# A decoder step with paged latent attention on one core: tiles that take a quarter of every page, and scales turned by VectorE

## The chip, the cores and the metric

The kernel runs on one core of a Trainium2 chip. The metric is the time of one execution on the device in microseconds (us). Everything is float32. Engines are named as in the profile: PE is TensorE (PEld its weight loads), DVE is VectorE, ACT is ScalarE, POOL is GpSimd, SP is SyncE, whose queue issues most DMAs.

## The reference

One step of a one-layer decoder serves 512 prompt tokens and 8 sample sequences of 4 tokens. It has two groups of heads: latent attention (MLA) and an RWKV-7 delta rule. The change touches only the attention of the sample tokens over a paged cache of latent rows:

```python
def _sample_attention(qn, qp, kn_new, kp_new, v_new, cache_ckv, cache_kpe, layer, page_table, w_ukv, g_kn):
    def step(carry, phys):
        c_blk = cache_ckv[layer, phys]
        kp_blk = cache_kpe[layer, phys]
        kn_blk, v_blk = _decompress(c_blk, w_ukv, g_kn)
        return _merge(carry, _attn_partial(qn, qp, kn_blk, kp_blk, v_blk, None)), None

    carry, _ = lax.scan(step, init, page_table.T)
```

`_decompress` multiplies a page's 128 latent rows of 256 numbers with `w_ukv` and normalises each head's 64 key numbers by their root mean square. A score is (query . normalised key + query . rotary key) x scale. The result is a softmax over 4096 cached and 4 new tokens, so the order of the tokens of a page does not matter, as long as all its users agree on it.

## The kernel before

The work over the cache ("page work") is 64 steps, `u`, each of four pages (512 tokens); eight steps in a row belong to one sequence. A step is cut in four slots, `t` = 0 to 3, and each engine has a generator (`pages_sp`, `pages_pool`, `pages_pe`, `pages_act`, `pages_dve`) that yields after each slot. The other work of the kernel (delta-rule chunks, sequence work, latent projections, prompt attention) calls `on_pe.go(n)`, `on_dve.go(n)` and so on between its own operations, which puts n slots of page work there into that engine's program. So the order on every engine is fixed by where `go` stands and by what a generator does in which slot; engines meet only at semaphores. 17 x 4 slots lie beside the chunks, 24 beside the sequence work, 35 beside the latent work, 34 beside the prompt attention (8 heads of four query tiles), and the last 91 run alone.

The way of one step:

- SP loads the pages into `c_ring` (`latent_pages`, L441), partition = token of the page; four steps fit the ring. From step 40 on POOL gathers two of the four pages (L489). SP waits for the landing, then copies 32 x 64 pieces into `blocks` (`blocks_of`, L451), half 0 (pages 0 and 1) and half 1 (pages 2 and 3), four copies each. A half is copied when its last transpose is done (`lo_sb`, `hi_sb`).
- DVE turns each half in 32x32 blocks into `c_T` (`turned_blocks`, L673): "lo" is half 0 (semaphore `lo_sb`), in slot 3 of the step before; "hi" is half 1 (`hi_sb`), in slot 0 of the step itself. It also turns the rotary keys `r_T` (L681, slot 1).
- PE computes the keys of one tile of 128 tokens per slot (`norms`, L563; tile t is page t), ACT squares them in PSUM (L609), DVE sums the squares per head (`reduce`, L686). `norms` of slot 0 waits for lo, that of slot 2 for hi, each for the sum two slots back.
- In slot 1 PE forms the dot products (`dots`, L526 with `r_T`, L530 with `c_T`), which wait for hi, and the value products of step u-2 (`values`, L547). ACT copies the latent part of the scores to SBUF (`dotted`, L604, slot 1).
- In slot 0 of the next step ACT and DVE make the 1/rms scales (`roots`, `scales`); DVE spreads them over `rep` (L696), in slot 2 PE turns them (`turn_scale`, L538), and DVE multiplies and adds (`score`, L705 to L712, slot 2). ACT takes the exponentials in slot 3 (`weights`, L624), PE turns them in slot 0 (L542), and DVE merges in slot 1 (`merge`, L718).

The norms are two matmuls a slot; a float32 matmul leaves two records in the trace, so a slot's norms are four records. The slots of VectorE (L726 to L738):

```python
            for u, t in slots:
                ahead = u + 1 < NSTEP
                if t == 0:
                    if u >= 1:
                        turned_blocks(u, 1)
                        scales(u - 1)
                if t == 1 and u >= 2:
                    merge(u - 2)
                if t == 2 and u >= 1:
                    score(u - 1)
                if t == 3 and ahead:
                    turned_blocks(u + 1, 0)
                reduce(u, t)
```

## Time and profile before

| | us |
|---|---|
| runs before: median of 3 (lowest, highest) | 1276.44 (1276.27, 1277.88) |
| the profiled execution's own time | 1276.86 |
| its span in the profile | 1275.1 |
| PE busy in the span | 1202.1 (94%) |
| DVE busy | 732.2 (57%) |
| ACT busy | 426.5 (33%) |
| POOL busy | 257.4 (20%) |

The profile is one execution, recorded by the hardware. A group of instructions shows its line, engine, operation and tiles, its busy time and count, the mean length of one in ns, and the idle time of the engine before them with what ended it. "issue" there means that the profile shows nothing that was waited for. Matmuls are pipelined, so a record's length overlaps the next one's; what an instruction takes from PE is the distance between starts. The granted clock of PE is given as a share of its full 2.4 GHz.

### The profile page before, as it was taken

What the parts mean: (1) busy time and instruction counts of PE and PEld (TensorE: products, weight loads), DVE (VectorE), ACT (ScalarE), POOL (GpSimd) and SP (SyncE); (2) the same over time, 40 slices, a digit from 0 to 9 for tenths busy, and PEclk for the clock granted to TensorE, in tenths of its full rate; (3) what the DMA queues carried; (4) which work ended last, traced back from release to release, by engine and by line L of the source; (5) the groups of instructions that cost most, each with busy time, mean ns of one, the idle gap of its engine ahead of it and who ended that gap; (6) DMA issues with size and microseconds to landing.
All of it is one profiled execution on the core that took longest, in us unless ns stands there. A gap on an engine that the chain in (4) does not pass through costs nothing. (4 is left out here: it accounts for less than half of the span.)

```text
span 1275.1 us, 23690 instructions
## 1 busy us (share of the span) xinstructions
PE 1202.1 (94%) x8783; PEld 661.3 (52%) x8783; DVE 732.2 (57%) x1801; ACT 426.5 (33%) x1041; POOL 257.4 (20%) x294
## 2 busy tenths in 40 slices
PE   6999999989999999999989988999999999989898
PEld 3545677745565565655434445555444444454343
DVE  4000437955667666774768787888676667430331
ACT  3000354323343333342444343333444444210310
POOL 0000134711011121234412340001323232000000
PEclk9999999999999999997999999999999999999999
DMA  6413112123232222351453226532576544101000
GB/s 219 168 55 87 35 33 67 53 59 80 66 81 67 76 73 77 84 115 42 124 143 88 76 74 171 168 80 74 153 184 172 139 122 123 50 1 38 17 21 33
DMA packets 205236, 114.45 MB, mean 90 GB/s; under 512 B 152977, under 2 KB 196433, under 8 KB 204994
## 3 DMA queue, kind: packets, MB, share of 16 engines
q1 hardware_dynamic: 198482, 96.56, 27.7%
q0 software_dynamic: 4352, 10.49, 3.3%
q10 hardware_dynamic: 2288, 5.89, 1.3%
q8 instruction: 70, 1.15, 0.4%
q14 instruction: 44, 0.36, 0.1%
HBM read 75.79 MB, written 4.07 MB: 63 GB/s over the span
## 5 line engine op out<-in xcount | busy, mean ns | idle before, releaser
L563 PE MATMUL PS<-wk,c_T 128*128 128x512 f32 x1024 | 494.5, 612 | 13.5 <-DVE c_T L673 12.4
L563 PEld LDWEIGHTS PS<-wk,c_T 128*128 128x128 f32 x1024 | 180.3, 193 | 207.8 <-issue 162.8
L686 DVE TENSOR_REDUCE ssq<-PS 128x8 f32<-128x512 f32 x256 | 176.3, 689 | 169.7 <-ACT PS L609 156.8
L609 ACT ACTIVATE PS<-PS 128x512 f32<-128x512 f32 x256 | 150.3, 587 | 271.8 <-PE PS L563 245.0
L1557 PE MATMUL PS<-xnT,w_ring 128*128 128x276 f32 x416 | 101.0, 400 | 0.0
L1395 PE MATMUL PS<-w_ring,xnT 128*128 128x424 f32 x256 | 96.4, 534 | 0.9 <-DVE xnT L1041 0.9
L673 DVE STREAM_TRANSPOSE c_T<-blocks 128x512 f32<-128x512 f32 x126 | 88.3, 701 | 3.7 <-DMA blocks<-c_ring 3.2
L1557 PEld LDWEIGHTS PS<-xnT,w_ring 128*128 128x128 f32 x416 | 77.8, 190 | 20.6 <-issue 4.1
L489 POOL DMA_INDIRECT c_ring<-in_cache_ckv,token_rows x48 | 45.3, 944 | 182.1 <-PE PS L547 174.8
L480 POOL DMA_INDIRECT r_ring<-in_cache_kpe,group_rows x64 | 62.0, 969 | 92.3 <-DVE r_T L681 68.0
L1395 PEld LDWEIGHTS PS<-w_ring,xnT 128*128 128x128 f32 x256 | 48.8, 194 | 45.5 <-issue 45.4
L2791 PE MATMUL PS<-w_g,nT 128*128 128x512 f32 x128 | 56.1, 595 | 0.0
L1347 POOL TENSOR_TENSOR diff<-cur 128x512 f32<-128x512 f32 x13 | 17.2, 1322 | 181.0 <-DVE cur_s L1256 171.9
L1049 DVE COPY nat<-PS 128x424 f32<-128x424 f32 x8 | 4.8, 597 | 75.2 <-PE PS L1395 75.2
L3069 ACT ACTIVATE pr<-PS,mx 128x128 f32<-128x128 f32 (+3 forms) x32 | 16.9, 527 | 73.0 <-DVE mx L2919 63.7
L530 PE MATMUL PS<-c_T,qp 128*32 128x128 f32 x1024 | 40.8, 275 | 0.3 <-issue 0.3
L547 PE MATMUL PS<-c_ring,ew 128*32 128x257 f32 x512 | 40.0, 382 | 0.1
L2791 PEld LDWEIGHTS PS<-w_g,nT 128*128 128x128 f32 x128 | 24.0, 190 | 30.4 <-issue 30.4
L1892 POOL TENSOR_TENSOR low<-raw_l,cst 128x512 f32<-128x512 f32 x12 | 12.8, 1093 | 121.6 <-ACT raw_l L1847 121.6
L526 PE MATMUL PS<-r_T,q_rope 128*32 128x128 f32 x512 | 27.5, 286 | 8.8 <-issue 8.7
L718 DVE SCALAR_TENSOR_TENSOR acc<-acc,ms,PS 128x257 f32<-128x257 f32 x64 | 30.5, 477 | 8.6 <-PE PS L547 8.4
L624 ACT ACTIVATE ew_q<-score_s,ms 128x128 f32<-128x128 f32 x64 | 32.8, 512 | 0.0
(535 smaller groups left out, 1725.3 us busy)
## 6 DMA issues: line engine op xcount, KB each, us to landing
blocks<-c_ring SPq DMA_DIRECT2D x504, 64.0 KB
c_ring<-in_cache_ckv SPq DMA_DIRECT2D x208, 128.0 KB, 2.2
w_ring<-in_w_in SPq DMA_DIRECT2D x4, 1696.0 KB, 12.4
w_ring<-in_w_in SPq DMA_DIRECT2D x9, 512.0 KB, 5.1
w_o<-in_w_out SPq DMA_DIRECT2D x8, 512.0 KB, 4.9
w_g<-in_w_ple_gate SPq DMA_DIRECT2D x8, 512.0 KB
xn<-in_x_prompt SPq DMA_DIRECT2D x4, 512.0 KB, 10.9
w_ring<-in_w_in SPq DMA_DIRECT2D x2, 1024.0 KB, 6.1
```

Of the source, the lines that this page charges most:

```text
L480: nc.gpsimd.indirect_dma_start(r_ring[:, u % R_RING, :], None, rows_of, bass.IndirectOffsetOnAxis(ap=group_rows[:, j * BS + b:j * BS + b + ...
L489: nc.gpsimd.indirect_dma_start(c_ring[:, u % RING, x, 0:KVL], None, io["cache_ckv"].rearrange("n p c -> (n p) c"), bass.IndirectOffsetOnAx ...
L530: mm = pe.matmul(PS[t * QH:(t + 1) * QH, TURN, at + P:at + 2 * P], qp[:, k, u // STEPS, :], c_T[:, u % 2, k, t * P:(t + 1) * P], start=(k ...
L547: mm = pe.matmul(PS[t * QH:(t + 1) * QH, MISC, at_v], ew[:, t * QH:(t + 1) * QH], c_ring[:, u % RING, t, :], start=True, stop=True)
L563: mm = pe.matmul(PS[:, NORM[v % 2], :], c_T[:, u % 2, k, t * P:(t + 1) * P], wk[:, k], start=(k == 0), stop=(k == 1))
L609: nc.scalar.activation(PS[:, NORM[v % 2], :], PS[:, NORM[v % 2], :], ACT.Square).then_inc(no_sb, 1)
L624: nc.scalar.activation(ew_q[:].rearrange("x (p s) -> x s p", s=GT), score_s[:, u % 2, :].rearrange("x (s p) -> x s p", s=GT), ACT.Exp, bia ...
L673: dve.transpose(c_T[:, u % 2, :, 2 * half * P:2 * (half + 1) * P].rearrange("d x (t s p) -> d s t x p", t=2, s=GT), blocks[:, half, :].rea ...
L686: dve.tensor_reduce(ssq[:, u % 2, t * H:(t + 1) * H], PS[:, NORM[v % 2], :].rearrange("p (h c) -> p h c", h=H), AX.X, ALU.add).then_inc(re ...
L1395: mm = pe.matmul(PS[:, u % 4, 0:w], xnT[:, k, i * P:(i + 1) * P], w_ring[:, c % 2, k, 0:w], start=(k == 0), stop=(k == KD - 1))
L1557: mm = pe.matmul(PS[:, 2 * (p % 2) + part, 0:t1 - t0], w_ring[:, wc % 2, k, at_:at_ + P], xnT[:, k, t0:t1], start=(k == 0), stop=(k == KD ...
L2791: mm = pe.matmul(PS[:, g_bank(i) + half, :], nT[:, i % 2, k, :], w_g[:, k, half * 512:(half + 1) * 512], start=(k == 0), stop=(k == KD - 1))
```

## The change

A tile of 128 tokens is now 32 tokens of each of the four pages (quarter t of every page), not one page. For that a page is loaded so that partition p holds token p % 4 * 32 + p // 4, and the gathers' row numbers follow; `c_T` is laid out by quarter, so every tile needs both halves of `blocks`. With tiles by quarter the scales need only be turned within 32x32 blocks: DVE does it (`scale_T`) and `turn_scale` is gone, as is ACT's copy `dotted` (DVE reads the dots from PSUM). The keys `r_T` and the latent columns of `dots` are read through rearranged patterns to match.

In the slots: both transposes of `blocks` for step u+1 now lie in slots 2 (lo) and 3 (hi) of step u; `norms` of slot 0 waits for both; `dots` waits for neither. `score` moves from slot 2 to slot 1, behind `merge`; `weights` on ACT from slot 3 to slot 2. The slots of SP and POOL are as they were.

```diff
--- before.py
+++ after.py
@@ -99,7 +99,7 @@
     parts += [("seq", (s // TS == np.arange(BS)[None, :]))]
     parts += [("headsum", (s // HN == np.arange(2)[None, :]))]
     parts += [("headones", (s // HN == t // HN))]
-    parts += [("lane", s % 32), ("token", s)]
+    parts += [("lane", s % 32), ("token", s % 4 * 32 + s // 4)]
     parts += [("mod32", (s % 32 == t % 32))]
     parts += [("causal", np.where(t <= s, 0.0, NEG))]
 
@@ -250,7 +250,7 @@
         rms = place("rms", [P, 2, GT * H])
         ssq = place("ssq", [P, 2, GT * H])
         score_s = place("score_s", [P, 2, P])
-        rep = place("rep", [P, GT * QH])
+        scale_T = place("scale_T", [P, P])
         ew_q = place("ew_q", [P, P])
         ew = place("ew", [P, GT * QH])
         ms = place("ms", [P, 4])
@@ -412,9 +412,9 @@
 
 
         (slot_taken, k_ps, k_sb, tn_sb, rp_ps, no_ps, no_sb, red_sb,
-         ri_sb, scale_sb, scale_ps, np_sb, top_sb, al_sb, eq_sb, ew_ps, ew_sb, vv_ps, acc_sb, dve_a) = kept_sems(*(
+         ri_sb, top_sb, al_sb, eq_sb, ew_ps, ew_sb, vv_ps, acc_sb, dve_a) = kept_sems(*(
             "slot_taken k_ps k_sb tn_sb rp_ps no_ps no_sb red_sb "
-            "ri_sb scale_sb scale_ps np_sb top_sb al_sb eq_sb ew_ps ew_sb vv_ps acc_sb dve_a").split())
+            "ri_sb top_sb al_sb eq_sb ew_ps ew_sb vv_ps acc_sb dve_a").split())
         c_in = [kept_sems(*(f"c_in{half}{x}" for x in range(RING))) for half in "ab"]
         block_in = kept_sems("block_in_a", "block_in_b")
         late_in = kept_sems("late_in_a", "late_in_b")
@@ -439,7 +439,7 @@
         def latent_pages(u, page):
             for x, number in enumerate(page):
                 nc.sync.dma_start(c_ring[:, u % RING, x, 0:KVL],
-                                  io["cache_ckv"][bass.ds(number, 1)].rearrange("o p c -> (o p) c")
+                                  io["cache_ckv"][bass.ds(number, 1)].rearrange("o (s g) c -> (o g) s c", s=GT)
                                   ).then_inc(c_in[x // 2][u % RING], 16)
 
         def blocks_of(u, half):
@@ -497,10 +497,10 @@
                 return R_RING
             return min(NSTEP, slot // GT + R_RING) + max(0, min(NSTEP, (slot + 6) // GT + 1) - GATHERED)
 
-        def by_token(k):
-
-            return (c_T[:, 0, k, :].rearrange("d (t s p) -> d t s p", t=GT, s=GT),
-                    PS[:, TURN, :].rearrange("d (t p s) -> d t s p", t=GT, s=GT))
+        def by_quarter(k):
+
+            return (c_T[:, 0, k, :].rearrange("d (s t g) -> d t s g", s=GT, t=GT),
+                    PS[:, TURN, :].rearrange("d (t g s) -> d t s g", s=GT, t=GT))
 
         def pages_pe():
             pe = nc.tensor
@@ -517,28 +517,24 @@
 
             def dots(u):
                 pe.wait_ge(tn_sb, u + 1)
-                if u >= 1:
-                    pe.wait_ge(hi_sb, u)
                 if u >= 2:
                     pe.wait_ge(top_sb, u - 1)
                 at = u % 2 * 2 * P
                 for t in range(GT):
-                    pe.matmul(PS[t * QH:(t + 1) * QH, TURN, at:at + P], q_rope[:, u // STEPS, t, :], r_T[:],
+                    pe.matmul(PS[t * QH:(t + 1) * QH, TURN, at:at + P], q_rope[:, u // STEPS, t, :],
+                              r_T[:].rearrange("d (s g) -> d g s", s=GT),
                               start=True, stop=True)
                 for k in range(2):
                     for t in range(GT):
                         mm = pe.matmul(PS[t * QH:(t + 1) * QH, TURN, at + P:at + 2 * P], qp[:, k, u // STEPS, :],
-                                       c_T[:, u % 2, k, t * P:(t + 1) * P], start=(k == 0), stop=(k == 1))
+                                       c_T[:, u % 2, k, :].rearrange("d (q t i) -> d t q i", q=GT, t=GT)[:, t],
+                                       start=(k == 0), stop=(k == 1))
                 mm.then_inc(rp_ps, 1)
 
-            def turn_scale(u):
-                pe.wait_ge(scale_sb, u + 1)
+            def turn_weights(u):
+                pe.wait_ge(eq_sb, u + 1)
                 if u >= 1:
                     pe.wait_ge(acc_sb, u)
-                pe.transpose(PS[:, MISC, at_t], rep[:], ident).then_inc(scale_ps, 1)
-
-            def turn_weights(u):
-                pe.wait_ge(eq_sb, u + 1)
                 pe.transpose(PS[:, MISC, at_t], ew_q[:], ident).then_inc(ew_ps, 1)
 
             def values(u):
@@ -555,8 +551,7 @@
                         pe.wait_ge(k_sb, 2)
                     else:
                         pe.wait_ge(lo_sb, u)
-                if t == 2 and u >= 1:
-                    pe.wait_ge(hi_sb, u)
+                        pe.wait_ge(hi_sb, u)
                 if v >= 2:
                     pe.wait_ge(red_sb, v - 1)
                 for k in range(2):
@@ -575,15 +570,12 @@
                     dots(u)
                     if u >= 2:
                         values(u - 2)
-                if t == 2 and u >= 1:
-                    turn_scale(u - 1)
                 norms(u, t)
                 yield
             turn_weights(NSTEP - 2)
             yield
             values(NSTEP - 2)
             yield
-            turn_scale(NSTEP - 1)
             yield
             turn_weights(NSTEP - 1)
             yield
@@ -595,13 +587,7 @@
 
             def turned_first():
                 act.wait_ge(k_ps, 1)
-                nc.scalar.copy(*by_token(0)).then_inc(k_sb, 1)
-
-            def dotted(u):
-                act.wait_ge(rp_ps, u + 1)
-                if u >= 2:
-                    act.wait_ge(eq_sb, u - 1)
-                nc.scalar.copy(score_s[:, u % 2, :], PS[:, TURN, u % 2 * 2 * P + P:u % 2 * 2 * P + 2 * P]).then_inc(np_sb, 1)
+                nc.scalar.copy(*by_quarter(0)).then_inc(k_sb, 1)
 
             def square(u, t):
                 v = u * GT + t
@@ -640,9 +626,7 @@
                         turned_weights(u - 2)
                     if u >= 1:
                         roots(u - 1)
-                if t == 1:
-                    dotted(u)
-                if t == 3 and u >= 1:
+                if t == 2 and u >= 1:
                     weights(u - 1)
                 square(u, t)
                 yield
@@ -666,11 +650,11 @@
 
             def turned_first():
                 dve.wait_ge(k_ps, 2)
-                dve.tensor_copy(*by_token(1)).then_inc(k_sb, 1)
+                dve.tensor_copy(*by_quarter(1)).then_inc(k_sb, 1)
 
             def turned_blocks(u, half):
                 dve.wait_ge(block_in[half], 64 * u)
-                dve.transpose(c_T[:, u % 2, :, 2 * half * P:2 * (half + 1) * P].rearrange("d x (t s p) -> d s t x p", t=2, s=GT),
+                dve.transpose(c_T[:, u % 2].rearrange("d x (s t g) -> d s t x g", s=GT, t=GT)[:, :, 2 * half:2 * half + 2],
                               blocks[:, half, :].rearrange("p (s t c x) -> p s t x c", s=GT, t=2, x=2)
                               ).then_inc((lo_sb, hi_sb)[half], 1)
 
@@ -687,22 +671,20 @@
                                   AX.X, ALU.add).then_inc(red_sb, 1)
 
             def scales(u):
-                wide = [P, GT * H, TS]
                 y, tmp = rms[:, 0, :], rms[:, 1, :]
                 dve.wait_ge(ri_sb, u * 2 + 2)
                 LA(dve.tensor_tensor(tmp, y, y, ALU.mult))
                 LA(dve.scalar_tensor_tensor(out=tmp, in0=ssq[:, u % 2, :], scalar=EPS * NOPE, in1=tmp, op0=ALU.add, op1=ALU.mult))
                 LA(dve.tensor_scalar(tmp, tmp, -0.5 / NOPE, 1.5, ALU.mult, ALU.add))
-                dve.tensor_tensor(rep[:].rearrange("p (x t) -> p x t", t=TS),
-                                  y.rearrange("p (x o) -> p x o", o=1).to_broadcast(wide),
-                                  tmp.rearrange("p (x o) -> p x o", o=1).to_broadcast(wide), ALU.mult).then_inc(scale_sb, 1)
+                LA(dve.tensor_tensor(tmp, y, tmp, ALU.mult))
+                LA(dve.transpose(scale_T[:], tmp.rearrange("p (x o) -> p x o", o=1).to_broadcast([P, GT * H, TS])))
 
             def score(u):
                 nm, sc, at = nmax[:, u // STEPS:u // STEPS + 1], score_s[:, u % 2, :], u % 2 * 2 * P
                 dve.wait_ge(rp_ps, min(u + 2, NSTEP))
-                dve.wait_ge(np_sb, u + 1)
-                dve.wait_ge(scale_ps, u + 1)
-                LA(dve.tensor_tensor(sc, sc, PS[:, MISC, at_t], ALU.mult))
+                if u >= 2:
+                    dve.wait_ge(eq_sb, u - 1)
+                LA(dve.tensor_tensor(sc, PS[:, TURN, at + P:at + 2 * P], scale_T[:], ALU.mult))
                 if u >= 1:
                     dve.wait_ge(eq_sb, u)
                 LA(dve.tensor_tensor_reduce(out=sc, in0=sc, in1=PS[:, TURN, at:at + P], scale=1.0, scalar=nm, op0=ALU.add,
@@ -725,16 +707,15 @@
             yield
             for u, t in slots:
                 ahead = u + 1 < NSTEP
-                if t == 0:
+                if t == 0 and u >= 1:
+                    scales(u - 1)
+                if t == 1:
+                    if u >= 2:
+                        merge(u - 2)
                     if u >= 1:
-                        turned_blocks(u, 1)
-                        scales(u - 1)
-                if t == 1 and u >= 2:
-                    merge(u - 2)
-                if t == 2 and u >= 1:
-                    score(u - 1)
-                if t == 3 and ahead:
-                    turned_blocks(u + 1, 0)
+                        score(u - 1)
+                if t >= 2 and ahead:
+                    turned_blocks(u + 1, t - 2)
                 reduce(u, t)
                 if t == 1 and ahead:
                     turned_r(u + 1)
```

Where the program's order changes, on DVE: a piece beside the prompt attention, from the end of slot 0 on. L2918 to L2934 (before) and L2899 to L2915 (changed) are the stage's own operations. Before:

```order
L2926 COPY prT<-PS 128x128
L718 SCALAR_TENSOR_TENSOR acc<-acc,ms,PS 128x257
L686 TENSOR_REDUCE ssq<-PS 128x8
L681 STREAM_TRANSPOSE r_T<-r_ring 128x128
L2930 RECIPROCAL mx<-mx 128x1
L2934 SCALAR_TENSOR_TENSOR nat<-PS,mx,nat 128x64
L2918 TENSOR_TENSOR PS<-PS,cst 128x128
L2919 TENSOR_REDUCE mx<-PS 128x1
L2926 COPY prT<-PS 128x256
L705 TENSOR_TENSOR score_s<-score_s,PS 128x128
L708 ISA score_s,ms<-score_s,PS,nmax 128x128
L708 ISA ms 128x1
```

Changed:

```order
L2907 COPY prT<-PS 128x128
L700 SCALAR_TENSOR_TENSOR acc<-acc,ms,PS 128x257
L687 TENSOR_TENSOR score_s<-PS,scale_T 128x128
L690 ISA score_s,ms<-score_s,PS,nmax 128x128
L690 ISA ms 128x1
L692 TENSOR_TENSOR ms<-ms,nmax 128x1
L694 COPY nmax<-ms 128x1
L670 TENSOR_REDUCE ssq<-PS 128x8
L665 STREAM_TRANSPOSE r_T<-r_ring 128x128
```

The score (L705 to L712 before, L687 to L694 now) stood in slot 2 behind `r_T` and the stage's operations; now it stands in slot 1, behind the merge and ahead of the slot's reduction.

On PE in the part that runs alone, with the semaphores waited for, from the norms of slot 0 to those of slot 2. Before:

```order
L563 MATMUL PS<-wk,c_T 128x512 [waits red_sb,lo_sb]
L563 MATMUL PS<-wk,c_T 128x512
L526 MATMUL PS<-r_T,q_rope 32x128 [waits top_sb,hi_sb,tn_sb]
L526 MATMUL PS<-r_T,q_rope 32x128 x3
L530 MATMUL PS<-c_T,qp 32x128 x8
L547 MATMUL PS<-c_ring,ew 32x257 [waits ew_sb]
L547 MATMUL PS<-c_ring,ew 32x257 x3
L563 MATMUL PS<-wk,c_T 128x512 [waits red_sb]
L563 MATMUL PS<-wk,c_T 128x512
L538 MATMUL PS<-cst,rep 128x128 [waits acc_sb,scale_sb]
L563 MATMUL PS<-wk,c_T 128x512 [waits red_sb,hi_sb]
```

Changed:

```order
L558 MATMUL PS<-wk,c_T 128x512 [waits red_sb,hi_sb,lo_sb]
L558 MATMUL PS<-wk,c_T 128x512
L524 MATMUL PS<-r_T,q_rope 32x128 [waits top_sb,tn_sb]
L524 MATMUL PS<-r_T,q_rope 32x128 x3
L529 MATMUL PS<-c_T,qp 32x128 x8
L543 MATMUL PS<-c_ring,ew 32x257 [waits ew_sb]
L543 MATMUL PS<-c_ring,ew 32x257 x3
L558 MATMUL PS<-wk,c_T 128x512 [waits red_sb]
L558 MATMUL PS<-wk,c_T 128x512
```

The scale transpose L538 is gone (L538 of the changed kernel is another line), the rope products no longer wait for `hi_sb`, and the norms of slot 0 do.

## Rows read from the trace of the kernel before

**Rows 1.** The view by stretches, three stages: busy us, instructions, clock, DMA.

```profile
265.00:560.00 295.00, 279.60 (x4086) 171.72 (x4087) 196.53 (x468) 106.66 (x251) 47.70 (x48) 0.98 0.31 78
560.00:765.00 205.00, 191.51 (x1230) 96.65 (x1230) 144.96 (x354) 84.33 (x229) 78.45 (x106) 0.96 0.34 91
765.00:897.00 132.00, 123.36 (x753) 72.03 (x754) 103.61 (x312) 49.59 (x154) 16.05 (x17) 1.00 0.44 124
```

**Rows 2.** Timeline of TensorE, 1000 to 1020 us: start, us, what, idle before.

```profile
1008.70 1.98 PE L563 MATMUL PS<-wk,c_T 128*128 128x512 f32 x4 [0.63 <-DVE c_T L673]
1010.62 0.43 PE L526 MATMUL PS<-r_T,q_rope 128*32 128x128 f32 x8
1010.86 0.62 PE L530 MATMUL PS<-c_T,qp 128*32 128x128 f32 x16
...
1011.84 1.98 PE L563 MATMUL PS<-wk,c_T 128*128 128x512 f32 x4
1013.66 0.27 PE L538 MATMUL PS<-cst,rep 128*128 128x128 f32 x1
1013.77 3.60 PE L563 MATMUL PS<-wk,c_T 128*128 128x512 f32 x8
...
1017.74 1.99 PE L563 MATMUL PS<-wk,c_T 128*128 128x512 f32 x4 [0.26 <-DVE c_T L673]
```

**Rows 3.** Timeline of VectorE, same stretch.

```profile
1015.31 0.25 DVE L705 TENSOR_TENSOR score_s<-score_s,PS 128x128 f32<-128x128 f32 x1
...
1016.99 0.70 DVE L673 STREAM_TRANSPOSE c_T<-blocks 128x512 f32<-128x512 f32 x1
```

**Rows 4.** SP's queue, timeline 903 to 1083 us; last row its waits (total, times, longest).

```profile
904.77 1.74 SPq L441 DMA_DIRECT2D c_ring<-in_cache_ckv  x2
...
1011.31 5.33 SPq L451 DMA_DIRECT2D blocks<-c_ring  x8
...
1072.65 0.86 SPq L441 DMA_DIRECT2D c_ring<-in_cache_ckv  x2
...
1081.52 0.87 SPq L441 DMA_DIRECT2D c_ring<-in_cache_ckv  x2
...
SPq L449 <- DMA c_ring<-in_cache_ckv: 26.7, 17, 2.2
```

**Rows 5.** Groups of TensorE, 265 to 560, then 640 to 765: busy, mean ns, idle before.

```profile
L563 PE MATMUL PS<-wk,c_T 128*128 128x512 f32 x301 | 147.3, 613 | 3.2 <-DVE c_T L673 3.0
...
L526 PE MATMUL PS<-r_T,q_rope 128*32 128x128 f32 x152 | 8.3, 292 | 2.0 <-issue 2.0
...
L526 PE MATMUL PS<-r_T,q_rope 128*32 128x128 f32 x64 | 3.4, 283 | 6.1 <-issue 6.1
```

**Rows 6.** Timelines of VectorE and of TensorE, 749 to 756 us.

```profile
753.71 0.70 DVE L673 STREAM_TRANSPOSE c_T<-blocks 128x512 f32<-128x512 f32 x1
...
754.51 0.42 PE L526 MATMUL PS<-r_T,q_rope 128*32 128x128 f32 x8 [3.50 <-issue]
```

**Rows 7.** Timelines in the attention, 815 to 832 us: VectorE, ScalarE, TensorE.

```profile
822.36 0.28 DVE L705 TENSOR_TENSOR score_s<-score_s,PS 128x128 f32<-128x128 f32 x1
...
823.45 0.69 DVE L686 TENSOR_REDUCE ssq<-PS 128x8 f32<-128x512 f32 x1
...
822.15 0.58 ACT L3069 ACTIVATE pr<-PS,mx 128x384 f32<-128x384 f32 x1 [2.33 <-issue]
...
822.72 0.59 ACT L609 ACTIVATE PS<-PS 128x512 f32<-128x512 f32 x1
825.74 0.69 ACT L3069 ACTIVATE pr<-PS,mx 128x512 f32<-128x512 f32 x1 [2.43 <-DVE mx L2919]
...
826.82 0.70 ACT L609 ACTIVATE PS<-PS 128x512 f32<-128x512 f32 x1
...
826.57 0.66 PE L2703 MATMUL PS<-cst,pr 128*128 128x128 f32 x4 [0.76 <-ACT pr L3069]
```

**Rows 8.** Groups of VectorE over the span: busy, mean ns, idle before.

```profile
L681 DVE STREAM_TRANSPOSE r_T<-r_ring 128x128 f32<-128x128 f32 x64 | 19.3, 301 | 1.9 <-DMA r_ring<-in_cache_kpe,group_rows 1.9
```

## The prediction

> **What bounds the kernel now.** I first read the page's busy shares, then the same by stage, then the waits of the stages that the change touches. TensorE is busy 93 to 95% of the stages before 897 us, VectorE 67 to 78% [rows 1]. So TensorE comes first, but its busy time hides short stalls, and each stage is looked at by itself. The page work (64 steps of four slots) runs from about 258 to 1099 us. It lies beside the delta-rule chunks (265 to 560), the sequence and latent work (to 765), the prompt attention (to 897), and then alone (to 1096). Three loops matter.
>
> (a) Alone, a step begins every 9.04 us: norms start at 1017.74, and at 1008.70 before it, after waiting for VectorE's lo transpose [rows 2]. Behind that wait stands a chain on VectorE: the score starts at 1015.31, one more reduction follows, and the lo transpose comes only at 1016.99 [rows 3].
>
> (b) In the same stage SP is hardly ever idle. It issues two pages in 0.87 us, waits for their landing (26.7 us over 17 steps, its only wait) and issues eight block copies in 5.33 us, then starts anew. From the page loads at 904.77 to those at 1081.52 there are 19 steps, so 9.30 us a step on average; the last of them, from 1072.65, takes 8.87 [rows 4]. The short one is below TensorE's 9.04, the average above it: steps in which SP also issues weight loads are longer. SP is at least as much the bound there as TensorE.
>
> (c) Before 897 TensorE stands still where VectorE is late. The clearest place is the first dot product of a step, which waits for the hi transpose in slot 0: 2.0 us beside the chunks and 6.1 us in the latent work [rows 5]. The profile puts this down to "issue", but the times tell: hi starts at 753.71 behind stage work and takes 0.70, and the dots start at 754.51 after 3.50 us of nothing [rows 6]. In the attention TensorE waits 0.76 us a head for ScalarE's exponentials [rows 7].
>
> **The change part by part.**
> *The scale transpose leaves TensorE* (64 of them). Its row says 0.27 us, but what it takes from the engine is the space from its start to the next start, 1013.77 - 1013.66 = 0.11 [rows 2]; the rest lies over its neighbours. There are 42 steps before SP becomes the bound; in the 8 beside the attention it is not in the loop that bounds. 34 x 0.11 = -3.7 us. (The Trainium skill, "VectorE: DVE Perf Modes", § The three transpose paths, gives TensorE's 128x128 transpose 390 ns, against 311 ns on VectorE, for bf16; at 390 ns the 34 would be worth 13 us and not 4. The spacing here speaks against that.)
>
> *VectorE pays for it.* The product that spread the scales over 128 columns goes; a product of 32 columns and a transpose of 128 (0.30 us, what r_T's takes, the same size) come [rows 8]. Since one product replaces another, that is at most 0.3 us more in slot 0, and I take 0.2, an estimate. ScalarE's copy of the dots goes. Slot 0 loses the hi transpose (0.70), so it still gets 0.5 lighter. The score (1.09 us from its start at 822.36 to the next reduction) [rows 7] moves from slot 2 to slot 1, in front of a reduction that waits for ScalarE anyway: 2 us between norms and their squares. I cost it at nothing; without that cover it would cost its 1.09 us. Slot 2 gets a transpose (about 0.65) for the score, 0.4 lighter.
>
> *hi moves from slot 0 to slot 3, and the dots' wait for it to the first norms.* hi now stands where lo stood, ahead of slot 0's stage work, and the norms waited there for lo already. The 8.1 us of the dots' waits [rows 5] go; some comes back, since the reduction of slot 0 still stands behind the same stage work and the third norms need it. I take 70%: -5.7 us. The shorter chain of (a) also helps before 897, where I take -2 us: beside the chunks alone norms waited 3.0 us for c_T [rows 5].
>
> *The attention.* Its loop runs norms of slot 1, square, VectorE, exponentials, TensorE. VectorE would come to its reduction of slot 2 0.4 us sooner (lo from 822.36 instead of a score that ends at 823.45). But the exponentials of the weights move from ScalarE's slot 3 to slot 2, behind the stage's exponential of 384 columns and ahead of the square. A square without them starts 822.72 - 822.15 = 0.57 after that one; with them 826.82 - 825.74 = 1.08 after one that is 0.11 longer. So the square starts 0.40 later and ends near 823.8, and the reduction with it, later than 823.45 [rows 7]. 8 heads x 0.4 = +3.2 us. If ScalarE did not matter it would be 8 x -0.4 = -3.5.
>
> *The stage alone.* With the score gone from slot 2, TensorE's loop runs over the norms of slot 2 (start 1013.77, 1.80 us), their square (0.6), the reduction (0.65) and hi (0.70): the next norms at 1017.5 instead of 1017.74, so 8.8 us a step instead of 9.04. But SP's 9.3 stays: its instructions are the same ones. The lo gate opens a little sooner, so SP's run may start some 0.7 us sooner; at the end the norms wait for the second half of the blocks instead of the first, 1.9 us more of TensorE's work behind the last landing. I take +0.5 us.
>
> *The page loads read with another pattern* (32 groups of four rows, each 1 KB, in place of 128 in a row). Nothing in the trace shows its issue. It has the same 128 pieces of 1 KB; the bounds are no change (0.43 us each) and the cost of a block copy (5.33/8 = 0.67) [rows 4]. I take none, nearest in piece size. At the upper bound: 2 x 0.24 x 22 steps = +10.6.
>
> *r_T is read with a stride.* The four rope products take their moving columns 32 elements apart. No TensorE row has a moving operand like it. They now take 0.24 us a step (1010.62 to 1010.86, the start of the next group). The bounds are 0 and the time in which four times as many columns pass, +0.72. I take 0: a record of 512 columns takes 0.45 us, 2.1 clocks a column at the full 2.4 GHz [rows 2], so a column need not come every clock. (The Trainium skill, "SBUF — State Buffer", in its note on cachelines, says that accesses which hit a new 16-byte line each time pay a penalty, and that 4 fp32 can be strided over for free; 32 are far beyond. No run here shows it yet; by it the rope products get slower.)
>
> Sum: -3.7 - 5.7 - 2 + 3.2 + 0.5 = -7.7 us. The profiled execution took 1276.9 (span 1275.1), 0.4 above the median of the runs, 1276.4. Taken from the median that gives **1268.7 us**.
>
> **The rivals.**
> *R1, the wait moves with the transpose.* hi in slot 3 holds the first norms as long as it held the dots, for VectorE has 0.2 us a step more to do and is busy 67 to 78% of these stages [rows 1]. Then -5.7 and -2 are gone: -3.7 + 3.2 + 0.5 = 0, 1276.4. Against it: at 753.71 the transpose stood behind stage work that it would now precede.
> *R2, strided rope reads cost three times the time* (the slower side). +0.48 x 42 = +20, so -7.7 + 20 = +12: 1289 us. It decides from the point where a step's rope products need over 0.42 us instead of 0.24 (7.7/42 is 0.18). Nothing in the rows speaks for it, the 2.1 clocks a column speak against it. (The line rule of the Trainium skill, "SBUF — State Buffer", is what speaks for it.) At twice the time it ends at +2.4, 1278.8.
> *R3, the page loads get dearer for SP,* each like a block copy: -7.7 + 10.6 = +2.9, 1279.3. For it: SP is where a step alone is bound. Against it: the pieces keep number and size.
> *R4, SP is not the bound alone:* the stage alone gets 22 x 0.2 = 4.4 faster and the attention does not lose: -7.7 - 4.4 - 3.2 = -15, 1261. Against it stands the 9.30 average.
> That the change doesn't do what it says is out: one transpose a step is gone from TensorE's order, and the score stands in slot 1.
>
> **How the numbers follow.** Forecast 0.53, R1 0.17, R2 at three times 0.09 and at twice 0.05, R3 0.08, R4 0.08. Measurements of this kernel can tell 0.2% (2.6 us) from no change. Faster: 0.53 + 0.08 + a little of R1 = 0.63; within: most of R1, much of R3 and of R2 at twice = 0.20; slower: the rest, 0.17. The range reaches from R4 over R3 to just beyond R2 at twice: 1260 to 1281; R2 at three times is left out.
>
> **What would show it.** Right: no idle before the rope products and none of "issue"; the rope group still 0.24 us; a step alone still 9.1 to 9.3 us with SP without a gap; page loads 0.43 us each; in the attention the wait before the stage's transposes as long as now or longer. Wrong: rope records longer than now, norms waiting for c_T before 897 as long as the dots did, or a step alone at 8.8 us, which would mean that SP had room.

## The result, and the profile after

The changed kernel takes 1303.16 us (median of 6 runs, 1297.41 to 1307.16); the kernel before, run beside it, took 1278.04 (6 runs, 1276.27 to 1283.69). The ratio is 1.0187, 95% interval 1.0154 to 1.0220: **slower, by about 25 us**. The forecast was 1268.7, its range 1260 to 1281. The profiled execution took 1307.16 us (span 1305.3), the longest of the six.

The page of the changed kernel, busiest groups. Line numbers have moved: L558 norms, L524 rope products, L529 latent products, L543 values, L657 the lo and hi transposes, L670 reductions.

```profile
PE 1215.1 (93%) x8719; PEld 668.2 (51%) x8719; DVE 748.0 (57%) x1865; ACT 411.0 (31%) x977; POOL 257.4 (20%) x294
L558 PE MATMUL PS<-wk,c_T 128*128 128x512 f32 x1024 | 495.3, 616 | 33.0 <-issue 25.9
L657 DVE STREAM_TRANSPOSE c_T<-blocks 128x512 f32<-128x512 f32 x126 | 87.4, 694 | 20.9 <-DMA blocks<-c_ring 20.8
```

The norms stand idle for 33.0 us, and VectorE's transposes wait 20.8 us for block copies. The groups of TensorE over the span show the dots:

```profile
L529 PE MATMUL PS<-c_T,qp 128*32 128x128 f32 x1024 | 45.6, 279 | 0.4 <-issue 0.4
L524 PE MATMUL PS<-r_T,q_rope 128*32 128x128 f32 x512 | 45.1, 423 | 0.0
```

The idle time before the rope products, which [rows 5] show, is gone as forecast. But one rope product takes 423 ns, where it took 283 to 292 [rows 5], while the latent products beside it take 279.

By stages, in the columns of [rows 1] (the last is the page work alone):

```profile
265.00:560.00 295.00, 281.28 (x4073) 172.29 (x4072) 202.12 (x491) 102.99 (x235) 47.62 (x48) 0.99 0.31 78
560.00:765.00 205.00, 192.57 (x1217) 97.66 (x1217) 148.80 (x368) 81.21 (x214) 78.64 (x106) 0.96 0.34 91
765.00:897.00 132.00, 120.54 (x700) 71.10 (x700) 102.20 (x307) 46.24 (x140) 13.22 (x14) 0.97 0.44 120
897.00:1096.00 199.00, 177.13 (x980) 78.02 (x979) 129.93 (x356) 70.06 (x177) 56.63 (x60) 1.00 0.51 136
```

Most of the loss has its place at the end: alone, TensorE is busy only 89% of the time (177.13 of 199), where it was busy 96% in the kernel before:

```profile
897.00:1096.00 199.00, 191.03 (x1097) 84.51 (x1096) 137.83 (x367) 83.67 (x218) 55.71 (x59) 1.00 0.56 142
```

Timeline of TensorE in the changed kernel there, 1040 to 1062 us, to be held against [rows 2]:

```profile
1045.77 1.96 PE L558 MATMUL PS<-wk,c_T 128*128 128x512 f32 x4 [1.15 <-issue]
1047.65 0.68 PE L524 MATMUL PS<-r_T,q_rope 128*32 128x128 f32 x8
1048.09 0.69 PE L529 MATMUL PS<-c_T,qp 128*32 128x128 f32 x16
...
1055.88 1.95 PE L558 MATMUL PS<-wk,c_T 128*128 128x512 f32 x4 [1.19 <-issue]
1057.76 0.71 PE L524 MATMUL PS<-r_T,q_rope 128*32 128x128 f32 x8
1058.21 0.70 PE L529 MATMUL PS<-c_T,qp 128*32 128x128 f32 x16
```

A step takes 10.11 us (1055.88 - 1045.77) instead of 9.04. From the first rope product to the first latent one go 0.44 us (1048.09 - 1047.65) instead of 0.24. And the norms start 1.15 to 1.19 us late, behind the hi transpose, which VectorE's timeline shows waiting for its DMA:

```profile
1044.96 0.71 DVE L657 STREAM_TRANSPOSE c_T<-blocks 128x512 f32<-128x512 f32 x1 [0.84 <-DMA blocks<-c_ring]
...
1055.07 0.71 DVE L657 STREAM_TRANSPOSE c_T<-blocks 128x512 f32<-128x512 f32 x1 [0.88 <-DMA blocks<-c_ring]
```

Those copies come from SP. Its timeline in the same stretch, and its wait between 903 and 1110 us:

```profile
1043.73 1.70 SPq L441 DMA_DIRECT2D c_ring<-in_cache_ckv  x2
1047.34 5.43 SPq L451 DMA_DIRECT2D blocks<-c_ring  x8
1053.93 1.39 SPq L441 DMA_DIRECT2D c_ring<-in_cache_ckv  x2
...
SPq L449 <- DMA c_ring<-in_cache_ckv: 34.1, 20, 2.5
```

The two page loads take 1.39 us of SP where they took 0.86 [rows 4]; a single one takes 0.60 instead of 0.34, with the same 128 pieces of 1 KB.

So two candidates stand out, and both are edits that the prediction costed at nothing: the order in which a page load reads, and the stride with which TensorE reads r_T. Both came with the tiles, but the tiles don't need them: with pages loaded row by row and r_T read in a row, score column 32s+g belongs to token 4g+s on both sides of the sum. The version with neither still computes the whole reference.

### The profile page after: what moved, and what is told of

Its sections match the earlier page's. It is cut to its first block and busy times, and to the rows that moved or that the text cites. A ratio compares the mean times of both kernels' runs of the same rounds, so it can differ in the third digit from the quotient of the medians.

```text
span 1305.3 us, 23499 instructions
## 1 busy us (share of the span) xinstructions
PE 1215.1 (93%) x8719; PEld 668.2 (51%) x8719; DVE 748.0 (57%) x1865; ACT 411.0 (31%) x977; POOL 257.4 (20%) x294
## 5 line engine op out<-in xcount | busy, mean ns | idle before, releaser
L558 PE MATMUL PS<-wk,c_T 128*128 128x512 f32 x1024 | 495.3, 616 | 33.0 <-issue 25.9
L558 PEld LDWEIGHTS PS<-wk,c_T 128*128 128x128 f32 x1024 | 181.1, 194 | 239.5 <-issue 213.9
L670 DVE TENSOR_REDUCE ssq<-PS 128x8 f32<-128x512 f32 x256 | 175.1, 684 | 129.0 <-ACT PS L595 119.3
L657 DVE STREAM_TRANSPOSE c_T<-blocks 128x512 f32<-128x512 f32 x126 | 87.4, 694 | 20.9 <-DMA blocks<-c_ring 20.8
L529 PE MATMUL PS<-c_T,qp 128*32 128x128 f32 x1024 | 45.6, 279 | 0.4 <-issue 0.4
L524 PE MATMUL PS<-r_T,q_rope 128*32 128x128 f32 x512 | 45.1, 423 | 0.0
L543 PE MATMUL PS<-c_ring,ew 128*32 128x257 f32 x512 | 43.5, 380 | 0.1
L529 PEld LDWEIGHTS PS<-c_T,qp 128*32 128x32 f32 x1024 | 39.5, 120 | 7.3 <-issue 0.7
```

Of the source, the lines that this page charges most:

```text
L524: pe.matmul(PS[t * QH:(t + 1) * QH, TURN, at:at + P], q_rope[:, u // STEPS, t, :], r_T[:].rearrange("d (s g) -> d g s", s=GT), start=True, ...
L529: mm = pe.matmul(PS[t * QH:(t + 1) * QH, TURN, at + P:at + 2 * P], qp[:, k, u // STEPS, :], c_T[:, u % 2, k, :].rearrange("d (q t i) -> d ...
L558: mm = pe.matmul(PS[:, NORM[v % 2], :], c_T[:, u % 2, k, t * P:(t + 1) * P], wk[:, k], start=(k == 0), stop=(k == 1))
L657: dve.transpose(c_T[:, u % 2].rearrange("d x (s t g) -> d s t x g", s=GT, t=GT)[:, :, 2 * half:2 * half + 2], blocks[:, half, :].rearrange ...
L670: dve.tensor_reduce(ssq[:, u % 2, t * H:(t + 1) * H], PS[:, NORM[v % 2], :].rearrange("p (h c) -> p h c", h=H), AX.X, ALU.add).then_inc(re ...
```

## The experiments

Four batches were run, each on one chip with the kernel before beside it. The chips differ by 0.7% (before took 1270.9, 1269.6, 1276.3 and 1278.3 us), so kernels of different batches are compared by their ratios. The unchanged kernel run as a kernel of its own gave 0.9983 (0.9969 to 0.9998), so a ratio can be trusted to about 0.2%.

Six versions (e1, e2, e4, e5, e11, e12) leave something out: each loads the pages or reads `r_T` in an order that the other does not match, so rotary keys meet the latents of other tokens and the scores of the cached tokens are not the reference's. Their instructions are the same in number and size. All the others compute the whole reference.

This table has all of them. The stretches are worked out from the timelines of the one profiled execution each: the starts of the first rope product of steps 0, 32 (beginning of the attention), 40, 44 (alone) and 63, and the end of the span. One execution is a small sample. The executions of one kernel in one batch lie up to 13 us apart, and the same kernel (e8 and e8b) has 472.6 and 483.4 us up to step 32 on two chips, so differences of a few us in that column say little. Steps 44 to 63 repeat within 2 us. The end varies from 182.7 to 186.1 us among kernels that all have the schedule of before (b0, e5, e4, e11, e12).

| kernel | ratio (95%) | 0-32 | 32-40 | 44-63 | end |
|---|---|---|---|---|---|
| before (first trace) | | 495.7 | 122.3 | 174.1 | 182.7 |
| b0_before_again | 0.9983 (0.9969-0.9998) | 485.3 | 123.5 | 174.5 | 182.7 |
| after (first trace) | 1.0187 (1.0154-1.0220) | 491.2 | 130.2 | 193.1 | 186.5 |
| a0_after_again | 1.0160 (1.0130-1.0191) | 489.0 | 129.0 | 191.3 | 185.0 |
| e1_pages_in_row | 1.0055 (1.0033-1.0077) | 480.8 | 128.6 | 180.6 | 184.8 |
| e2_rope_in_row | 1.0069 (1.0050-1.0089) | 473.1 | 127.0 | 189.1 | 183.0 |
| e3_both_in_row | 0.9975 (0.9956-0.9995) | 474.1 | 126.5 | 180.0 | 184.7 |
| e5_before_rope | 1.0097 (1.0072-1.0121) | 494.6 | 125.6 | 177.3 | 182.9 |
| e6_weights_slot3 | 0.9956 (0.9933-0.9980) | 469.8 | 125.2 | 178.7 | 184.4 |
| e7_numbers_early | 0.9966 (0.9948-0.9984) | 473.9 | 126.4 | 176.1 | 186.1 |
| e8_pages_between | 0.9929 (0.9912-0.9946) | 472.6 | 126.5 | 171.8 | 186.4 |
| e4_before_pages | 1.0106 (1.0077-1.0135) | 489.9 | 125.7 | 185.5 | 184.4 |
| e9_all_three | 0.9936 (0.9912-0.9960) | 480.0 | 125.1 | 171.7 | 184.6 |
| e10_hi_in_slot3 | 1.0054 (1.0029-1.0078) | 483.1 | 132.9 | 176.0 | 184.4 |
| e11_stride_4 | 1.0123 (1.0082-1.0164) | 500.2 | 125.5 | 178.4 | 184.6 |
| e12_stride_2 | 1.0005 (0.9984-1.0027) | 490.6 | 123.8 | 174.7 | 186.1 |
| e8b_again | 0.9939 (0.9916-0.9962) | 483.4 | 126.4 | 172.3 | 186.1 |
| e9b_again | 0.9940 (0.9920-0.9961) | 480.4 | 125.1 | 172.9 | 186.4 |

### Batch 1: which of the two patterns costs

e1 has the pages in a row (and the token constant of before), e2 has r_T in a row, e3 both; e5 is the kernel before with the strided read of r_T alone.

```diff
-  io["cache_ckv"][bass.ds(number, 1)].rearrange("o (s g) c -> (o g) s c", s=GT)   # e1, e3
+  io["cache_ckv"][bass.ds(number, 1)].rearrange("o p c -> (o p) c")
...
-  r_T[:].rearrange("d (s g) -> d g s", s=GT),                                     # e2, e3; e5 the other way
+  r_T[:],
```

e1_pages_in_row: 

> The changed kernel, but each page is loaded as before, 128 rows in a row (and the gathers' rows likewise); the rope products still read r_T with a stride, so that rotary keys meet latents of other tokens. Theory A (the page pattern costs SP 0.26 us an issue and a longer landing, 1 us a step where a step runs alone; the strided rope read costs TensorE 0.2 us a step beside the other stages): a step alone falls from 10.1 to 9.1 to 9.3 us, page issues from 0.60 to 0.34 us, the time from 1303 to 1281 to 1284. Rival B (the wait for both halves before the first norms costs the time, whatever the pattern): a step alone stays near 10 us, the time above 1295.

e2_rope_in_row: 

> The changed kernel, but the rope products read r_T's columns in a row (rotary keys meet latents of other tokens); the pages are loaded in the new pattern. Theory A: the rope group falls from 0.44 to 0.24 us a step, a step alone stays at 10.1 us since SP sets it there, and only the 42 steps before gain: 8 us, 1303 to 1295. Rival B (the rope read is hidden): 1303, nothing. Rival C (it is most of the loss): 1280 or below.

e3_both_in_row: 

> The changed kernel with both old patterns: pages loaded in a row, r_T read in a row; tokens of all tiles agree again. What is left of the change is the scale transpose on VectorE, tiles by quarter and the new slots. Theory A (the two patterns are the whole loss, and the rest is worth what was forecast): 1269 to 1273, below the kernel before by 5 to 8 us; a step alone 9.1 to 9.3 us. Rival B (the waits moved, the rest is worth nothing): 1276 to 1279. Rival C (the earlier wait for both halves costs time): 1282 or more.

e5_before_rope: 

> The kernel before with one edit: the rope products read r_T through the changed kernel's strided pattern (rotary keys meet latents of other tokens). Theory A: the rope group takes 0.44 instead of 0.24 us; each step of 64 gets 0.2 us longer where TensorE's loop sets it, the loop alone from 9.04 to 9.24: 8 to 13 us in all, 1286 to 1291. Rival B (the stride costs only through the changed slots): 1278.

**Both cost, and about the same.** The changed kernel stands at 1.0187 and 1.0160; with one pattern taken back it stands at 1.0055 or 1.0069, and with both at 0.9975. On the kernel before, the stride alone costs 1271 x 0.0097 = 12.3 us, or 0.19 us for each of 64 steps. On the changed schedule the kernels of this batch, run on one chip, give a second price each. e1 and e3 differ by the stride alone: 10.5 us by the medians (1278.40 against 1267.87), of which the traces show 6.7 up to step 32 and only 0.6 in steps 44 to 63. e2 and e3 differ by the page pattern alone: 11.6 us (1279.50 against 1267.87), of which 9.1 lie in steps 44 to 63. The rope groups of e5 and of e2 over the span show that the stride alone makes the record long:

```profile
L526 PE MATMUL PS<-r_T,q_rope 128*32 128x128 f32 x512 | 45.4, 426 | 8.4 <-issue 8.1 <-DVE r_T L682 0.3
```

```profile
L524 PE MATMUL PS<-r_T,q_rope 128*32 128x128 f32 x512 | 27.5, 287 | 0.0
```

The expectations were in microseconds beside a kernel before of 1278; on this chip it takes 1271, so the ratios count. e2 came out well below its theory A (1.0069, not 1295 / 1278 = 1.013): the stride had been given too small a share of the loss and the pages too large a one. What is left of the change, e3, is worth 3 us, less than the 7.7 that the prediction gave it and between its theory A and rival B. The steps alone of e1 and e3 take 9.5 us on average (180.6 and 180.0 over 19), above the 9.1 to 9.3 of theory A; batch 2 asks why.

### Batch 2: what holds e3 back

Against b0_before_again, which ran on another chip, e3 gains 11.2 us up to step 32 (474.1 against 485.3), but gives back 3.0 in the attention, 5.5 in the steps alone and 2.0 at the end. Alone, its steps vary from 8.88 to 10.3 us. This is the timeline of TensorE in e3:

```profile
1023.43 1.96 PE L558 MATMUL PS<-wk,c_T 128*128 128x512 f32 x4 [0.91 <-issue]
...
1033.25 1.96 PE L558 MATMUL PS<-wk,c_T 128*128 128x512 f32 x4 [1.16 <-issue]
...
1042.34 1.95 PE L558 MATMUL PS<-wk,c_T 128*128 128x512 f32 x4 [0.43 <-issue]
```

And this is its SP, whose one wait is for the landing of the pages:

```profile
1023.87 6.36 SPq L451 DMA_DIRECT2D blocks<-c_ring  x8
1031.10 0.86 SPq L441 DMA_DIRECT2D c_ring<-in_cache_ckv  x2
1033.75 5.32 SPq L451 DMA_DIRECT2D blocks<-c_ring  x8
```

e6 and e7 are each e3 with one more edit, and e8 is e7 with one more. e6 moves ScalarE's `weights` back to slot 3. e7 lets SP read the next page numbers (0.6 us a step) behind the page loads instead of ahead of them. e8 also issues the next pages before the last of the eight copies, from step 44 on.

```diff
-                if t == 2 and u >= 1:            # e6
+                if t == 3 and u >= 1:
                     weights(u - 1)
```

```diff
-                page = page_numbers(u)           # e7
...
                     latent_pages(u, page)
+                if u + 1 < NSTEP:
+                    page = page_numbers(u + 1)
```

```diff
+                        blocks_of(u, 1, range(3))            # e8
+                        sp.wait_ge(vv_ps, u + 1 - RING + 1)
+                        latent_pages(u + 1, page)
+                        blocks_of_last(u)
```

b0_before_again: 

> The kernel before, unchanged, for a trace from the same chip as the three runs beside it. Ratio 1.000 (0.998 to 1.002). Mean step alone from the rope products of step 44 to those of step 62: 9.1 to 9.3 us.

e6_weights_slot3: 

> The changed kernel with both access patterns in a row (the whole computation; e3_both_in_row) and ScalarE's exponentials of the weights back in slot 3. Theory A (the attention term of the prediction: in slot 2 they hold the square back by 0.4 us a head, 8 heads, and the score leaving slot 2 was worth as much): 3 to 6 us under e3, a ratio to before of 0.993 to 0.995. Rival B (the exponentials have room in either slot, TensorE in the attention does not wait longer for them): the same as e3, 0.9975 within 0.001.

e7_numbers_early: 

> e3_both_in_row, and SP reads the page numbers of the next step right behind the page loads, while it would wait for their landing anyway, instead of in front of the next page loads. Theory A (alone, SP is the bound: its step there is issue 0.92 + landing 2.06 + block copies 5.62 + rest 0.92 = 9.52 us): the 0.6 us of number reads vanish in the landing wait, the step alone falls to 8.9 us, 22 x 0.6 = 13 us at most, 8 to 13 us under e3, ratio to before 0.987 to 0.991. Rival B (VectorE and TensorE set the step alone at 9.2 to 9.5 and SP only follows): the same as e3, 0.9975 within 0.001, and SP's wait for landing simply grows.

e8_pages_between: 

> e7_numbers_early, and from step 44 on the pages of the next step are issued before the last of a step's eight block copies, so that a copy covers part of their landing. Theory A (SP still the bound at e7): SP's step alone loses another 0.6 us, but TensorE's own loop of 8.8 us takes over: 0 to 3 us under e7. Rival B (the page loads now wait for the values' products of three steps before, and the last block copy with them): the hi transposes come later, the step alone grows to 9.3 to 9.8 us, and the kernel is 5 to 15 us slower than e7.

**SP is what stretches the steps alone.** With its number reads hidden, steps 44 to 63 take 176.1 us instead of 180.0 (178.7 in e6, which ran on the chip of e7); with part of the landing hidden too they take 171.8, below the 174.5 of before. That is less than theory A expected of e7 (4 us, not 8 to 13; the landing wait grew from 2.06 to 2.57 us a step, and its ratio can't be told from e3's). Of e8 theory A expected 0 to 3 us under e7 and it gave 4.8; rival B's longer steps did not come. The timeline of TensorE in e8 shows the loop that then bounds:

```profile
1026.39 1.95 PE L572 MATMUL PS<-wk,c_T 128*128 128x512 f32 x4 [0.29 <-issue]
...
1035.26 1.96 PE L572 MATMUL PS<-wk,c_T 128*128 128x512 f32 x4 [0.22 <-issue]
...
1044.14 1.10 PE L572 MATMUL PS<-wk,c_T 128*128 128x512 f32 x2 [0.22 <-issue]
```

The steps are 8.87 us (1035.26 - 1026.39), as against the 8.8 that the prediction worked out for TensorE's loop; 12 of its last 21 take 8.87 or 8.88. e6 lies 0.0019 under e3 by the ratios, 2.4 us, between its two theories; their intervals overlap, so it decides nothing.

### Batch 3: the parts on the kernel before

e4 is the kernel before with the changed page pattern (the first change of batch 1's diff and the token constant, the other way). e10 is the kernel before with its hi transposes in slot 3, behind the reduction. e9 joins e6, e7 and e8.

```diff
                     if u >= 1:                  # e10, VectorE, slot 0
-                        turned_blocks(u, 1)
                         scales(u - 1)
...
                 reduce(u, t)
+                if t == 3 and ahead:
+                    turned_blocks(u + 1, 1)
```

a0_after_again: 

> The changed kernel, unchanged, on the chip of the three runs beside it. Ratio to before 1.0187 within 0.004 (1.015 to 1.023). Step alone 10.1 us, rope products to latent products 0.44 us.

e4_before_pages: 

> The kernel before with the changed kernel's access pattern for the page loads (32 groups of four rows) and nothing else; the latents then stand at other tokens than the rotary keys. Theory A (the pattern costs SP 0.26 us an issue, two a step, and a landing a little longer; SP is the bound of the step alone): the step alone goes from 9.2 to 9.8 to 10.0 us, 22 x 0.7 = 15 us, ratio 1.008 to 1.014. Rival B (only the changed kernel's schedule makes SP so tight): within 3 us of before, ratio under 1.003.

e9_all_three: 

> The changed kernel with both access patterns in a row, ScalarE's weights in slot 3 (e6), the page numbers read in the landing wait (e7) and, from step 44 on, the next pages ahead of the last block copy (e8); the whole computation. Theory A (the attention's wait and SP's are separate): e8 less the 3 to 5 us that e6 took from e3, 1254 to 1257 us where before is 1269.6, ratio 0.988 to 0.990. Rival B (they overlap): as e8, 0.993.

e10_hi_in_slot3: 

> The kernel before, with the hi transposes moved on VectorE from the start of slot 0 to the end of slot 3, behind its reduction, so that only the other stages' work of the slot stands behind them now; tiles, scores, TensorE's scale transpose stay. Theory A (the dots' wait for hi is what the change gains before 897 us): 6 to 9 us by step 40, ratio 0.993 to 0.996. Rival B (the gain comes from the transpose and the score that left): within 2 us of before, ratio 0.998 to 1.001.

**The page pattern costs 1.06% by itself**, 1276.3 x 0.0106 = 13.5 us, as theory A said. It costs most where SP is short: 11.0 us in steps 44 to 63 (185.5 against 174.5, or 0.58 a step). Timelines of e4 there, SP first, then TensorE, whose norms now wait 1.0 to 1.5 us for the lo transpose:

```profile
1037.34 5.44 SPq L451 DMA_DIRECT2D blocks<-c_ring  x8
1043.65 1.39 SPq L441 DMA_DIRECT2D c_ring<-in_cache_ckv  x2
...
1033.09 1.98 PE L563 MATMUL PS<-wk,c_T 128*128 128x512 f32 x4 [1.48 <-DVE c_T L673]
...
1043.25 1.98 PE L563 MATMUL PS<-wk,c_T 128*128 128x512 f32 x4 [1.01 <-DVE c_T L673]
```

**e10 was a miss for both theories**: it is slower than before. The wait that it was meant to remove is gone. Rope and norms groups of TensorE, 265 to 765 us, in e10 (in b0_before_again the same rope row has 8.1 us of idle time, and the norms 5.1):

```profile
L563 PE MATMUL PS<-wk,c_T 128*128 128x512 f32 x522 | 256.7, 618 | 4.9 <-DVE c_T L673 4.6
L526 PE MATMUL PS<-r_T,q_rope 128*32 128x128 f32 x256 | 13.6, 285 | 0.2 <-issue 0.2
```

Up to step 32 it is 6.8 us faster than e4 on the same chip (483.1 against 489.9; e4 may pay for its pages there too, so this is an upper bound). But steps 32 to 40, in the attention, take 132.9 us where e4 takes 125.7 and the two traces of before 122.3 and 123.5. TensorE's waits in e10 between 765 and 897 us:

```profile
PE PS L2704 <- ACT pr L3070: 5.9, 8, 0.9
PE PS L2704 <- DVE prT L2927: 3.9, 7, 0.6
```

The first is in b0_before_again as well (5.9). The second is new: the stage's copies of `prT` stand behind a VectorE slot that now has the lo and the hi transpose. That this slot is what delays them is read from the order, not tried. e9 gave 0.9936, not the 0.988 to 0.990 of its theory A but its rival B's 0.993.

### Batch 4: why the stride costs, and ScalarE's slot

e11 and e12 read r_T on the kernel before with the stride of a line and of half a line.

```diff
                     pe.matmul(PS[t * QH:(t + 1) * QH, TURN, at:at + P], q_rope[:, u // STEPS, t, :],
-                              r_T[:],
+                              r_T[:].rearrange("d (g s) -> d s g", s=4),     # e11; s=2 in e12
```

e11_stride_4: 

> The kernel before, with the rope products' moving columns read four elements (16 bytes) apart, in four runs of 32, instead of in a row; the rotary keys then meet the latents of other tokens. The changed kernel reads them 32 elements apart in 32 runs of four, which on the same kernel gave 0.447 us from the first rope product to the first latent one and a ratio of 1.0097. Theory A (the price is a new 16-byte line at every element): 0.44 us, ratio 1.007 to 1.012. Rival B (the price is the short inner run, or the long jump): 0.24 to 0.28 us, ratio 0.998 to 1.002.

e12_stride_2: 

> As e11_stride_4, but two elements (8 bytes) apart, in two runs of 64, so that two elements in a row share a 16-byte line. Theory A (a new line at every element is what costs; the Trainium skill, SBUF - State Buffer, in the note on cachelines, wants at least two hits on a line): 0.24 us from rope to latent products, ratio 0.998 to 1.002. Rival C (any stride above one costs): 0.3 to 0.45 us, ratio 1.003 to 1.010.

e8b_again: 

> e8_pages_between once more, beside e9b. Ratio to before 0.991 to 0.995.

e9b_again: 

> e9_all_three once more, on one chip with e8b; they differ in the slot of ScalarE's exponentials of the weights alone (2 in e8b, 3 here). Theory A (the attention term of the prediction, 0.4 us a head): 3 us under e8b, and between steps 32 and 40 of the page work 3 us less. Rival B (no more than the 1.3 us that the traces of e3 and e6 differ by between those steps): within 2 us of e8b.

Four elements apart, in runs of 32, the rope products cost what they cost 32 apart in runs of four: 0.444 us to the first latent product, on the mean of 64 steps, against 0.447 in e5. Two elements apart it is 0.254, against 0.242. The rows of e11 and e12 over the span:

```profile
L526 PE MATMUL PS<-r_T,q_rope 128*32 128x128 f32 x512 | 41.1, 401 | 8.2 <-issue 8.1
```

```profile
L526 PE MATMUL PS<-r_T,q_rope 128*32 128x128 f32 x512 | 28.1, 290 | 8.3 <-issue 8.1
```

So it is neither the short run nor the long jump: **the price was paid with each fp32 16 or 128 bytes from the last, and not with 8 bytes between them.** The Trainium skill, "SBUF — State Buffer", has in its note on cachelines (§ Door 1: The DMA port swizzle) lines of 16 bytes and at least two hits on a line for the full rate, and these rows agree with both. The same note lets 4 fp32 be strided over for free. If that means a stride of 4, e11 measured otherwise: at a stride of 4 the whole price was paid, and at 2 almost none. e8b and e9b differ by nothing (0.9939 and 0.9940); by their traces steps 32 to 40 differ by 1.3 us. Rival B.

## Why the prediction was wrong

Two costs that it put at nothing, the strided read of `r_T` and the new pattern of the page loads, made the loss. The other terms came to a gain, as forecast, but of 3 us and not 7.7.

**What bounds the kernel.** View (a), TensorE's loop of 9.04 us, was right. View (b), that SP is "at least as much the bound", was wrong in degree. In the first trace of before, 16 of the last 21 steps take 9.03 to 9.05 us by their rope products, so TensorE's loop sets most of them; in b0_before_again it is 11 of 21. e5 and e11, which lengthen that loop alone, confirm it: 20 of 21 steps take 9.30 to 9.33 in e5, and 14 of 21 take 9.25 to 9.27 in e11. SP's average of 9.30 came from four of its 19 steps, of 9.90 to 10.35 us; the other 15 take 9.07 on average. SP was close behind, without room.

**"r_T is read with a stride ... I take 0": the step that failed, first.** It cost 12.3 us on the kernel before and 10.5 on the changed schedule (e1 less e3). Per step it is 0.20 us, within the bounds of 0 and 0.72. The reason given for 0 was that a record of 512 contiguous columns takes 2.1 clocks a column, "so a column need not come every clock". A record's length says nothing of strided reads. The rope products of a step are over 0.24 us after they start, with records of 283 to 292 ns each [rows 5], so the four of them overlap, and a row with one operand in a row had no word on what they need. (Whether a lone strided product would cost as much was not tried.) The Trainium skill's line rule was cited against the edit and outvoted by an inference from a row of another kind. R2 was the right mechanism. Its main form, three times the time, was too large (0.48 a step), but at twice the time, 0.24 x 42 = +10, it came close to both measured prices. The count of steps depends on the kernel: on the kernel before the steps alone pay too (177.3 in e5 against 174.1 to 174.7 in before, b0 and e12), while on the changed schedule with plain page loads they hardly do (0.6), since SP is what they wait for. (With the new page pattern too, after and a0 take 2 to 4 us more there than e2, on other chips.)

**"The page loads ... I take none, nearest in piece size": failed as well.** It cost 13.5 us on the kernel before and 11.6 on the changed schedule (e2 less e3). SP's issue rose by 0.26 us a page, the upper bound of 0.24 a little exceeded, so R3 at 10.6 us was about right. The number and size of the pieces stayed; the order in which they are read from the page did not.

**The two were treated as alternatives.** R2 and R3 each had a small chance of its own, and no case held both. Together they come to 12.3 + 13.5 = 25.8 us on the kernel before. With e3's -3.2 (1271 x 0.0025) that gives +22.6, where the two measurements of the changed kernel gave +20 and +24 (1276.3 x 0.0160, 1278.0 x 0.0187). The prices on the changed schedule come to a little less: -3.2 + 10.5 + 11.6 = +18.9. The range ended at 1281, since R2 at three times was left out.

**Before the attention: right in sum, by terms that were each off.** The scale transpose, hi and the shorter chain were put at -3.7 - 5.7 - 2 = -11.4 us. Against b0 on the same chip, e7 is 11.4 shorter up to step 32, e8 12.7 and e6 15.5; against e12 on another, e9b is 10.2 and e8b 7.2 shorter. The forecast lies within these, and that it meets e7's to the tenth is luck. TensorE's idle time from 265 to 765 us, in b0 and then in e7, shows the terms:

```profile
L563 PE MATMUL PS<-wk,c_T 128*128 128x512 f32 x523 | 257.5, 618 | 5.1 <-DVE c_T L673 4.8
L526 PE MATMUL PS<-r_T,q_rope 128*32 128x128 f32 x264 | 14.4, 289 | 8.1 <-issue 8.1
L538 PE MATMUL PS<-cst,rep 128*128 128x128 f32 x32 | 9.8, 305 | 1.6 <-DVE acc L718 1.6
...
L560 PE MATMUL PS<-wk,c_T 128*128 128x512 f32 x532 | 261.8, 619 | 7.0 <-issue 3.8 <-DVE c_T L659 1.8 <-DVE ssq L672 1.4
L526 PE MATMUL PS<-r_T,q_rope 128*32 128x128 f32 x264 | 14.3, 289 | 0.0
```

The wait before the rope products went whole (-8.1, where 70% of it, -5.7, was taken). The norms' idle time grew by 1.9, about the 30% that the prediction let come back; nothing is left to show for the -2 of the shorter chain. The scale transposes were worth more: the 32 before 765 us stood 0.14 us from the next start on average, not 0.11, and behind 1.6 us of waiting, 32 x 0.14 + 1.6 = 6.1. Of hi alone e10 says up to 6.8. Its ratio agrees: e10 is 6.9 us slower than before as a whole, its stretches from step 32 on are 13.1 us longer than those of b0, and that leaves about 6 for the steps before.

**The attention: right in size, its cause right in part.** +3.2 was forecast, and e3 and e7 lose 3.0 and 2.9 in steps 32 to 40 against b0. The wait that the prediction named did grow. TensorE's waits for ScalarE's exponentials from 765 to 897 us are 5.9 in before and in b0; in e3, and then in e6, which has `weights` back in slot 3:

```profile
PE PS L2684 <- ACT pr L3050: 7.9, 7, 1.3
...
PE PS L2684 <- ACT pr L3050: 5.5, 13, 0.8
```

But of the 3 us that slot makes 1.3 (e3 against e6, e8b against e9b), and nothing that the medians of e8b and e9b show. The rest was not traced to a cause. e10 shows a larger danger: hi in slot 3, behind lo and the reduction, costs 7 us there against e4 and 9 against b0 when the score still stands in slot 2. The change puts lo in slot 2 and the score in slot 1, and that may be why it loses only 3; neither was tried alone.

**The stage alone: mis-sized.** +0.5 was forecast for the version without the two patterns; e3 loses 5.5 in steps 44 to 63 and 2.0 at the end, against b0. Whether the 1.9 us "behind the last landing" are in this 2.0 can't be told: e2, which has the changed slots, ends in 183.0 us, and e12, which has those of before, in 186.1. The loss in steps 44 to 63 is SP's: in e3 its step is 9.43 us on average (page loads at 907.70 to those at 1068.06, 17 steps) and TensorE's could be 8.87. e7 and e8 show that SP is the cause, as they give the time back. A likely reason, argued only: the norms waited for the lo half before, that is for the fourth copy, and now wait for the eighth, so less stands between a late SP and TensorE. Whether SP's own step really grew from 9.30 to 9.43 stays open (it is 9.28 in b0 and 9.36 in e6).

**A version that beats both.** e8 takes 0.9929 and 0.9939 of the time before on two chips, e9 0.9936 and 0.9940: quarter tiles, both patterns in a row, SP's number reads behind its page loads, and in the steps alone its page loads one copy earlier. That is 8 to 9 us under the kernel before and about 30 under the changed one.

## What to carry to other kernels

Where a change permutes tiles, follow the permutation through the sum before adding patterns that undo it: here the plain page load and the plain r_T already agreed. An access pattern that no row shows is not free because its bytes are the same; try it on the old kernel alone, one run each. When two unknown costs stand in one change, give their sum a case of its own. And a queue whose average step is near the bound should be read step by step, not by its mean.
